# Seven half-size products for the upper half of two output projections and for one pair of value projections, sums added to h by quarters

## The reference

```python
h = x
# layer 0
h = h + mlstm_mixer(h, a_norm, a_w_in, ...)       # ends in  y @ a_w_out   (1024 x 1024)
h = h + conv_ffn(h, f_norm[0], f_w_up[0], ...)
kb, vb = shared_kv(h, kv_norm, w_kv, ...)         # rmsnorm(h) @ w_kv      (1024 x 2048)
# layer 1
h = h + moba_mixer(h, b_norm, b_w_q, ..., b_w_o, kb, vb, ...)   # ends in  o @ b_w_o
h = h + conv_ffn(h, f_norm[1], f_w_up[1], ...)
# second block, two layers
x = x + gate * rmsnorm(concat(conv * silu, attention * silu) @ w_out, g_post)
```

## Time and profile before

| | us |
|---|---|
| median of 3 runs | 979.46 (979.26 to 980.17) |
| the profiled execution's own time | 979.17 |
| its span | 977.4 |
| PE busy | 964.8 |
| DVE busy | 696.7 |
| ACT busy | 275.9 |

### The profile page before, as it was taken

One profiled execution on the slowest core, in us unless ns is written; L12 is line 12 of the kernel. 1 busy time (PEld: TensorE's weight loads), 2 busy tenths in 40 slices (PEclk: granted clock), 3 DMA queues, 4 the chain that ended last, 5 costly groups with the idle time before them and its releaser, 6 DMA issues.

```text
span 977.4 us, 15502 instructions
## 1 busy us (share of the span) xinstructions
PE 964.8 (99%) x5899; PEld 869.5 (89%) x5899; DVE 696.7 (71%) x1490; ACT 275.9 (28%) x596; POOL 1.1 (0%) x8
## 2 busy tenths in 40 slices
PE   9999999999999999999999999999999999999997
PEld 8878989999999988888899999999888878888876
DVE  5668648886788488644478768875799972799963
ACT  2132111111111222254121121112433363634461
POOL 0000000000000000000000000000000000000000
PEclk9999999999999999999999999999999999999999
DMA  9991475766776240692357667762743512533201
GB/s 274 283 292 37 174 222 183 258 240 210 262 259 234 75 141 1 203 362 82 120 175 261 231 228 250 267 220 91 228 169 130 162 44 84 192 120 116 65 1 44
DMA packets 133111, 170.84 MB, mean 175 GB/s; under 512 B 8755, under 2 KB 120643, under 8 KB 132931
## 3 DMA queue, kind: packets, MB, share of 16 engines
q1 hardware_dynamic: 131155, 167.69, 52.2%
q10 hardware_dynamic: 1904, 2.45, 0.7%
HBM read 168.93 MB, written 2.64 MB: 176 GB/s over the span
## 4 chain that ended last, share of the span: by engine, by line
PE 89%; DVE 9%; ACT 1%; issue 1%; DVEq 0%; POOL 0%; POOLq 0%
PE bank L1335 26%; PE bank L1348 16%; PE bank L1019 9%; PE bank L1651 5%; DVE work L2362 4%; PE bank L1106 4%; PE bank L1445 4%; PE bank L1030 3%; PE bank L1311 3%; PE bank L1637 2%; PE bank L1113 2%; PE bank L1543 2%; PE bank L1562 2%; PE bank L1486 1%; PE bank L1078 1%
## 5 line engine op out<-in xcount | busy, mean ns | idle before, releaser
L1348 PE MATMUL bank<-work,fring 128*128 128x256 f32 x704 | 155.6, 379 | 0.0
L1348 PEld LDWEIGHTS bank<-work,fring 128*128 128x128 f32 x704 | 132.1, 190 | 17.0
L2144 DVE SCALAR_TENSOR_TENSOR work<-work,cols 128x256 f32<-128x256 f32 x176 | 71.6, 480 | 53.3 <-ACT work L704 53.3
L2362 DVE SCALAR_TENSOR_TENSOR work<-work,cols 128x256 f32<-128x256 f32 x240 | 98.8, 482 | 1.6 <-ACT work L877 1.1
L1335 PE MATMUL bank<-sq,fring 128*128 128x128 f32 x640 | 84.5, 275 | 0.0
L704 ACT ACTIVATE work<-work,cols 128x256 f32<-128x256 f32 x88 | 45.8, 591 | 122.1 <-DVE work L2123 100.8
L1335 PE MATMUL bank<-sq,ring 128*128 128x128 f32 x640 | 78.0, 275 | 0.0
L1335 PE MATMUL bank<-ring,fring 128*128 128x128 f32 x640 | 78.0, 275 | 0.0
L1335 PEld LDWEIGHTS bank<-sq,fring 128*128 128x128 f32 x640 | 77.9, 192 | 0.0
L1335 PEld LDWEIGHTS bank<-ring,fring 128*128 128x128 f32 x640 | 76.2, 192 | 1.0
L1335 PEld LDWEIGHTS bank<-sq,ring 128*128 128x128 f32 x640 | 74.7, 192 | 0.0
(11 more groups left out here) (383 smaller groups left out, 1521.6 us busy)
## 6 DMA issues: line engine op xcount, KB each, us to landing
fring<-in_f_w_up SPq DMA_DIRECT2D x44, 1024.0 KB, 7.5
work<-in_w_ada SPq DMA_DIRECT2D x32, 768.0 KB, 6.0
fring<-in_f_w_down SPq DMA_DIRECT2D x22, 1024.0 KB, 4.8
ring<-in_w_in SPq DMA_DIRECT2D x18, 1024.0 KB, 5.2
ring<-in_a_w_in SPq DMA_DIRECT2D x10, 1024.0 KB, 11.8
ring<-in_w_kv SPq DMA_DIRECT2D x8, 1024.0 KB, 6.0
ring<-in_w_out SPq DMA_DIRECT2D x8, 1024.0 KB, 4.9
ring<-in_a_w_out SPq DMA_DIRECT2D x4, 1024.0 KB, 9.8
```

The lines of the kernel that those rows point to most:

```text
L1348: last = mm(pb[m // 2][:, T * (m % 2):T * (m % 2 + 1)], w[:, k, P * m:P * (m + 1)], f_act[:, par, T * k:T * (k + 1)], start=(first and k = ...
L2144: ins = v.scalar_tensor_tensor(f_t[q][:, c, :], f_u[:, q, c, tap:tap + T], col(f"f_conv_w{f}", 44 * tap + n), f_t[q][:, c, :], ALU.mult, A ...
L2362: marks[c] = link(v.scalar_tensor_tensor(b_y[:, c, :], b_a[:, c, tap:tap + T], col("conv_w_2", 124 * l + 4 * tap + c), b_y[:, c, :], ALU.m ...
```

## The change

- **Output projections** (`out_pair`): slots 12 and 13 (and 28, 29) stay full products. Slots 14 and 15 (and 30, 31) become seven products per column half, 28 matmuls of 128 tokens for each half. DVE first makes the sums of x (`out_x_terms`) and of the weights (`out_weight_terms`), then `out_half` adds the products straight to the quarters of chunks 4 to 7 of `hT`: first chunks 4 and 6, then 5 and 7. ACT copies each first product between the squares of h. `up_plain` takes the chunks in the order 0, 1, 2, 3, 4, 6, 5, 7.
- **Values**: slots 24 and 25 become a fourth pair of seven products. Its weight sums start in the middle of `pair_sums(2)`, its additions (`pair_sums(3)`) come after the queries' rotation, and ACT's scaled copy (`pair_scaled(3)`) after the copies of the turned heads. SP loads slots 28 to 31 ahead of the second FFN's weights, and those wait for the fourth pair (`tok_out` 20 in place of 16).
- **mLSTM**: DVE reads the gates before it scales the keys, and adds the first value products (`v_out(0)`) after the whole gate chain; ACT's `v_first_out(1)` comes before `v_scaled(0)`; only the first of the four weight sums of pair 3 stays ahead of `m_probs(3)`.
- **Attention of the second block**: the reciprocal of head 0 comes ahead of its taps, those of heads 5 and 6 ahead of the last third of their taps, that of head 7 ahead of the sum for the mean.

```diff
@@ constants
+        OUT_PAIR = ((14, 15), (30, 31))
+        OUT_PAIR_BANK = ((2, 3, 3), (4, 5, 0))
+        OUT_CHUNKS = (0, 1, 2, 3, 4, 6, 5, 7)
...
@@ sync
-            for n in range(20, 28):
+            for n in range(20, 32):
                 load(n)
-            product(sp, 23)
-            sp.wait_ge(S("tok_out"), 16)
+            product(sp, 25)
+            sp.wait_ge(S("tok_out"), 20)
             for i in (0, 1):
                 load_up(1, i, 1 - i)
                 load_down(1, i, 1 - i)
-            for n in range(28, 36):
+            for n in range(32, 36):
                 load(n)
...
@@ scalar
                 for m in range(4):
+                    x = hT[:, 2 * m:2 * m + 2, :]
+                    if first_of_half is not None and m >= 2:
+                        first_of_half(m - 2)
+                        x = hT[:, 2 + m:8:2, :]
                     act.wait_ge(S("h_ready"), 4 * k + m + 1)
...
@@ tensor
-            for m in range(1, 4):
-                feat(12 + m, pb[m], m_y)
+            def out_pair(f, x):
+                val, gate = [slot8(n) for n in OUT_PAIR[f]]
+                x11, x12, x21, x22 = quarters(x)
+                for c in range(2):
+                    one, two, end = [pb[n] for n in OUT_PAIR_BANK[c]]
+                    p = 2 * (1 - c)
+                    for i, bank, at, w, side in ((0, one, 0, val[:, 0:4], x11), (1, one, 1, val[:, 4:8], x21),
+                                                 (2, one, 2, s_2[f], o_t[1]),
+                                                 (3, two, 0, s_1[f], o_t[0]), (4, two, 1, gate[:, 0:4], o_t[2]),
+                                                 (5, end, p, s_last[f], x22), (6, end, p + 1, gate[:, 4:8], o_t[3])):
...
+                        if c == 0 and i == 2:
+                            arrived(pe, OUT_PAIR[f][1])
+                            pe.wait_ge(S("t_ready"), (2, 6)[f])
+                            pe.wait_ge(S("s_ready"), (6, 21)[f])
+                        if c == 1 and i == 5:
+                            pe.wait_ge(S("h_ready"), (5, 13)[f])
+                        for k in range(4):
+                            last = mm(bank[:, P * at:P * (at + 1)], w[:, k, P * c:P * (c + 1)], side[:, k, :],
+                                      start=(k == 0), stop=(k == 3))
...
+            feat(13, pb[1], m_y)
+            pe.wait_ge(S("m_raw"), 8)
+            out_pair(0, m_y)
...
             pe.wait_ge(S("m_raw"), 10)
-            token(24, pb[0], xg)
-            token(25, pb[1], xg)
+            pair_of(3, lambda: pe.wait_ge(S("p1_out"), 33), None)
...
-            pe.wait_ge(S("tok_out"), 20)
+            pe.wait_ge(S("m_raw"), 12)
...
@@ vector
+            def out_half(f, c):
+                one, two, end = [pb[n] for n in OUT_PAIR_BANK[c]]
...
+                dve.wait_ge(S("p1_out"), (8, 34)[f] + c + 1)
+                n = link(v.tensor_tensor(three(W(a, a + T), 2), p1.unsqueeze(1).broadcast_to([P, 2, P]),
+                                         three(one[:, P:3 * P], 2), ALU.add))
...
+                if c == 0:
+                    dve.wait_ge(S("seven_done"), (4, 15)[f])
+                else:
+                    dve.wait_ge(S("out_five"), f + 1)
...
+                if c == 1:
+                    product(dve, OUT_PAIR[f][1])
+                v.tensor_tensor(h1, h1, end[:, P * p:P * (p + 1)], ALU.add)
+                v.tensor_tensor(h2, h2, end[:, P * (p + 1):P * (p + 2)], ALU.add).then_inc(S("h_ready"), 1)
...
-            for m in range(4):
+            out_x_terms(0, m_y)
+            out_weight_terms(0)
+            for m in range(2):
                 product(dve, 12 + m)
                 add_pair(m, pb[m])
                 gained(1, xg, "f_norm", "xg_ready", pairs=[m])
                 if m == 0:
                     s_forms(1, 1)
+            for c in range(2):
+                out_half(0, c)
+                gained_chunks(1, c, 0)
...
             attention(0, A_DH ** -0.5, lambda n: pc("mask_ts", DIAG))
             layer_gains(0)
-            product(dve, 27)
+            out_weight_terms(1)
             s_forms(0, 7)
+            out_x_terms(1, a_oT)
...
```

More of the change, by code:

```diff
@@ L312, in slot8, with quarters @@
             return slot(n).rearrange("p (k n) -> p k n", k=8)
+        OUT_PAIR = ((14, 15), (30, 31))
+        OUT_PAIR_BANK = ((2, 3, 3), (4, 5, 0))
+        OUT_CHUNKS = (0, 1, 2, 3, 4, 6, 5, 7)
+        OUT_RAW = (8192, 9216)
+        o_t = [ring[:, 3, 512 * i:512 * i + 512].rearrange("p (k n) -> p k n", k=4) for i in range(4)]
+        def quarters(x):
+            return x[:, 0:4, 0:P], x[:, 0:4, P:T], x[:, 4:8, 0:P], x[:, 4:8, P:T]
         gain_all = slot(56)[:, 0:D]
@@ L1514, in _ @@
             heads_out((6, 7)).then_inc(S("product"), 1)
-            for m in range(1, 4):
-                feat(28 + m, pb[m], a_oT)
+            feat(29, pb[1], a_oT)
+            out_pair(1, a_oT)
             ffn(1, 3)
@@ new lines, in out_x_terms @@
+            def out_x_terms(f, x):
+                x11, x12, x21, x22 = quarters(x)
+                if f == 0:
+                    dve.wait_ge(S("m_y_done"), 4)
+                else:
+                    dve.wait_ge(S("o_out"), 8)
+                product(dve, (11, 27)[f])
+                n = link(v.tensor_tensor(o_t[0], x12, x11, ALU.subtract))
+                v.tensor_tensor(o_t[2], x22, x12, ALU.subtract)
+                after(n)
+                then(v.tensor_tensor(o_t[1], x22, o_t[0], ALU.subtract))
+                v.tensor_tensor(o_t[3], x21, o_t[1], ALU.subtract).then_inc(S("t_ready"), 1)
@@ L1843, in _, with m_first_sum @@
                                     a_norm_cols[:, 2 * m + c:2 * m + c + 1], None, ALU.mult).then_inc(S("xg_ready"), 1)
[L1844 to L1846 removed]
+            def m_first_sum(p):
+                gate = slot8(M_PAIRS[p][1])
                 for n in M_PAIRS[p]:
@@ L1926, in _ @@
             v.tensor_copy(rcol[:, 1:2], pb[2][:, P:P + 1]).then_inc(S("rcol_done"), 1)
-            for c in range(2):
-                dve.wait_ge(S("m_raw"), c + 1)
-                v.tensor_tensor(W(1024, 2048).rearrange("p (j c t) -> p j c t", j=2, c=2)[:, :, c, :],
-                                three(W(K_RAW[c], K_RAW[c] + 512), 2), rbc2, ALU.mult).then_inc(S("m_k_out"), 1)
-            v_out(0)
             dve.wait_ge(S("m_gate_proj"), 1)
@@ L2323, in attention @@
                         between(n)
+            pair_sums(3)
             attention(0, A_DH ** -0.5, lambda n: pc("mask_ts", DIAG))
             layer_gains(0)
-            product(dve, 27)
+            out_weight_terms(1)
             s_forms(0, 7)
-            for m in range(4):
+            out_x_terms(1, a_oT)
+            for m in range(2):
                 product(dve, 28 + m)
@@ L2332, in _ @@
                 gained(3, xg, "f_norm", "xg_ready", at=DC, pairs=[m])
+            for c in range(2):
+                out_half(1, c)
+                gained_chunks(3, c, DC)
             ffn(1, 3, 6)
@@ L2471, in layer, with reciprocals @@
                 masked_bias(0)
-                for n_head in range(9):
-                    if n_head >= 1:
-                        dve.wait_ge(S("exp_done"), 2 * (8 * (1 + l) + n_head))
-                        at = 140 + 2 * ((n_head - 1) % 2)
-                        v.reciprocal(sml[:, at + 4:at + 6], sml[:, at:at + 2]).then_inc(S("recip_done"), 1)
+                def reciprocals(n_head):
+                    dve.wait_ge(S("exp_done"), 2 * (8 * (1 + l) + n_head + 1))
+                    at = 140 + 2 * (n_head % 2)
+                    v.reciprocal(sml[:, at + 4:at + 6], sml[:, at:at + 2]).then_inc(S("recip_done"), 1)
+                for n_head in range(8):
                     if n_head < 8:
```

164 lines of the change are left out of this document (111 added, 53 removed).

## The result

Twelve runs of each kernel: 974.15 us median with the change (971.64 to 977.86), 979.85 without (979.15 to 981.75), a ratio of 0.9934 with a 95% interval of 0.9923 to 0.9946. The profiled execution of the changed kernel took 971.93 us with a span of 970.1, against 979.17 and 977.4 before: 7.2 us less. In a second measurement the changed kernel had a median of 971.81 (6 runs, ratio 0.992, 0.9904 to 0.9937).

The account below looks back on a forecast made before the run. PE, busy 99% of the span, was taken as the bound. Terms of -2.62 (projections), -0.58 (values), -2.84 (mLSTM) and -0.75 (second block) sum to -6.79 us, put at 972.6; range 970.6 to 975.0.

Parts of the forecast that it names:

- first output projection: On PE, 64 wide records (13.81 us) become 112 narrow ones (12.50 us), 1.31 us shorter.
- second output projection: The same replacement of wide by narrow records in the later projection, 1.31 us shorter, with more room at its join.
- values pair, net: Slots 24 and 25 as seven products save 1.73 us; ACT's scaled copy before the first exponential costs 1.15; net -0.58.
- mLSTM, gates: PE's 1.38 us gap until DVE has read the gates out of bank 7 goes.
- mLSTM, last probabilities: PE's 1.46 us gap before head 3, where m_probs(3) ran behind four weight sums, goes.
- reciprocals: Second block's attention: earlier reciprocals shorten PE's waits for ACT's scaling of probabilities; -0.75 us, bounds 0 and -2.66.
- The price of a product: PE's time per record: 0.2158 us for 256 tokens, 0.1116 for 128, so half the tokens cost 0.517.
- The joins: Handovers around the output projections: sums ready in time, no cost taken, bounds -0.3 and +0.6 us each.
- the rival of 974.6: Late first-product copy or last quarter of h stalls PE about 1 us at each projection; chance 0.13.
- the rows of head 7: Second block: head 7's reciprocal waits for ACT's exponential, whose maximum keeps its place on DVE, limiting the gain to 0.75 us.
- SP's queue: Second FFN's first weights, requested about 427.3 instead of 408.9, still land in time: no cost, 8 us of slack.
- that rival: Late second-FFN weights hold up PE in the second output projection; 987.1 us at a third of the load pace, chance 0.02.

Follow-up runs that it names:

- recip_undone: The changed kernel with the second block's reciprocals again behind DVE's taps, as in the kernel before; 973.86 us.
- weights_late6: The changed kernel with the second FFN's first six weight slots requested only when head 5 of the first attention is done; 985.05 us, ratio 1.0054 to the kernel before.

## Why the prediction was right, and where not

The forecast was 972.6 with a range of 970.6 to 975.0; the median came to 974.15 and to 971.81. Neither lies within 971.9 to 973.6, to which the prediction gave 0.53. The 974.15 is inside the range by luck: its upper end was meant for late joins, and there were none. What was right are the mechanism and the sum, as PE's positions before and after show it. The terms, in us, beside the kernel that undoes each:

| term | predicted | in the trace | undone alone |
|---|---|---|---|
| first output projection | -1.31 | -1.31 | |
| second output projection | -1.31 | -1.31 | +1.29 |
| values pair, net | -0.58 | -0.86 | +0.86 |
| mLSTM, gates | -1.38 | -1.45 | +1.45 |
| mLSTM, last probabilities | -1.46 | -1.45 | +1.43 |
| reciprocals | -0.75 | -0.78 | +0.77 |
| sum | -6.79 | -7.16 | |

- **The price of a product** held without a remainder: 0.1116 us a narrow record, with no idle between the new ones. The Trainium skill (TensorE: Matmul & The Clock Gate, Back-to-back issue gap) gives some 81 ns a matmul at 128 columns for a stream of loads and multiplies; if each of these records is two passes, as the prediction estimated, a pass takes 55.8 ns, and the trace does not agree with the page, in 224 new records as in the 56 of the earlier trace rows.
- **The joins** cost nothing, as forecast: the rival of 974.6 failed on slacks that were real (4.18 measured where 4.3 was worked out). The median lies near that rival's number by accident; the trace after has no wait at a join. One reading was wrong without harm: the second projection has not more room than the first but less, since the x sums end at 457.25 and PE's third product starts at 460.56, 3.3 us.
- **The values** are the one term that was mis-sized, by 0.28 us. The step that failed is "the exponential could start at 426.07 and starts at 427.22, 1.15 late". It started 0.87 later than the gain would have allowed, for two reasons, both of reading durations as distances: I took the end of the four turned copies (start plus 2.43) for the start of what follows, and that comes 2.29 behind (421.35 - 419.06), as ACT's instructions overlap; and I took 1.37 for the scaled copy from start to start, where it is 1.23 (422.58 - 421.35).
- **mLSTM**: both gaps closed whole, 2.90 at PE. Taking the whole gap was right because in both places the row named one releaser, whose place on DVE moved by more than the gap.
- **The second block**: -0.52 in the first layer and -0.26 in the second. Staying with the rows of head 7 was right: `recip_undone` shows 1.5 us of waits that were worth 0.77. What I said of the waits left holds in the pace: head 7 has a new one in both layers (0.3 each as listed, 0.47 each in the pace), and head 1 a gap of 0.23 that the view does not list.
- **SP's queue** cost nothing, and `weights_late6` shows that this was slack and not luck: with the request 23 us later, DVE waited 12.6 us for the slot and the whole kernel lost 11. The price of that rival was too low in the prediction, which counts a late slot by its own length: the clock that fell while PE stood took 1.6 us more.
- **The level.** In the lower group the kernel is 0.7 us better than the forecast, by the values' 0.28, the few hundredths of the other terms, a start 0.15 earlier and the 0.2 by which the forecast was put above the profiled execution's sum. The first measurement's median is 1.55 above the forecast because two thirds of its executions lie in the upper group or above; that they lost 1.7 us to the clock in the mLSTM is likely from the traces of the other kernels, and not shown for this one. The prediction took one profiled execution as the level of all; its range had no term for that.

## What to carry to other kernels

When one engine is 99% busy, a change is a sum: its own time taken out, gaps closed, gaps opened, and PE's own terms and the closed gaps can be read from the pace of its rows to within a tenth of a us; the gap that opened was 0.28 off. An instruction that the change puts on another engine has a place as well as a length: two copies ahead of an exponential cost half of what the pair had saved, and nothing 2 us later, so after every such change look at what stands ahead of the first link of a chain that PE waits for. Waits that follow each other on one chain are not added up: five of them with 2.1 us became two with 0.6, and that was worth 0.8.

## What the runs showed of the hardware

- With PE standing for 9.3 us its granted clock went from 1.00 to 0.50 (2.4 to 1.2 GHz), and the 24 records after it took 4.26 us in place of 2.68. A stall of that length costs more than its length.
- The clock also fell to 0.50 for some 3.4 us with PE busy by its own rows, in the same place of the mLSTM in five profiled executions, before the change and after it, and not in nine others. It costs 1.7 us, which is more than any term of this change: a single median of a dozen runs can be off by that, and a comparison of PE's positions with the stretch taken out is not.
- Instructions that follow each other on ACT overlap: four copies of 128x512 on ACT, listed with 2.42 us, are followed by the next instruction 2.29 behind their start, and two scaled copies, listed with 1.34, 1.23 behind theirs. Not everywhere: the scaled pair of the earlier trace rows, listed with 1.34 at 407.53, is followed 1.37 behind its start.
